# Hybrid attention block: value projection and gates moved into stages of their own, the head turns cut from 24 to 16 units

## What is computed

```python
h = rms_norm(x, norm_mix)
proj = h @ w_in            # q, k, v of 8 "diff" heads, then q, k, v of 8 "fox" heads, then 8 forget logits
# diff: two 64-wide q/k maps a head, each RMS-normed; p = softmax(q1 k1 + alibi) - lam * softmax(q2 k2 + alibi)
#       out = rms_norm(p @ v) * (1 - lambda_init)
# fox:  q and k RMS-normed over 128; logits q k + F[t] - F[s], F = cumsum(log_sigmoid(f_logit + b_forget))
gates = sigmoid(h @ w_gate + b_gate)                       # 2 x 2048 columns
merged = g_diff * (oa @ w_branch_diff) + g_fox * (ob @ w_branch_fox)
x = x + merged @ w_out
h2 = rms_norm(x, norm_mlp)
x = x + relu(h2 @ w_mlp_up) ** 2 @ w_mlp_down              # hidden width 8192
```

## Time and profile before

| what | value |
|---|---|
| time, median of 3 runs | 2764.06 us (2763.19 to 2764.08) |
| the profiled execution's own time | 2764.29 us |
| its span, from the first to the last instruction | 2762.6 us |
| PE busy in it | 2740.2 us, 99% of the span |
| DVE busy | 1704.2 us, 62% |
| ACT busy | 1114.0 us, 40% |
| granted TensorE clock, mean | 0.999 |
| head turns, from the trace | 28.8 to about 695 us, 83.4 us a turn |

### The profile page before, as it was taken

One profiled execution on the slowest core, in us unless ns is written; L12 is line 12 of the kernel. 1 busy time (PEld: TensorE's weight loads), 2 busy tenths in 40 slices (PEclk: granted clock), 3 DMA queues, 4 the chain that ended last, 5 costly groups with the idle time before them and its releaser, 6 DMA issues.

```text
span 2762.6 us, 42063 instructions
## 1 busy us (share of the span) xinstructions
PE 2740.2 (99%) x14920; PEld 2369.3 (86%) x14920; DVE 1704.2 (62%) x2924; ACT 1114.0 (40%) x1565; POOL 39.9 (1%) x65
## 2 busy tenths in 40 slices
PE   8999999999999999999999999999999999999999
PEld 7888888888888888888889999999998888888887
DVE  5666766667655555563478788788874444444443
ACT  5444444444322222233344444444454334334343
POOL 1000000000000000010000000000000000000000
PEclk9999999999999999999999999999999999999999
DMA  5333232222233333334523443434347565565653
GB/s 161 77 77 76 76 76 75 76 73 80 84 92 99 98 94 97 99 103 131 163 95 127 134 130 123 137 127 132 128 148 251 186 229 195 184 232 192 214 203 115
DMA packets 382059, 358.36 MB, mean 130 GB/s; under 512 B 13299, under 2 KB 302134, under 8 KB 382006
## 3 DMA queue, kind: packets, MB, share of 16 engines
q1 hardware_dynamic: 366534, 332.45, 39.0%
q10 hardware_dynamic: 15472, 25.20, 2.4%
HBM read 332.44 MB, written 25.17 MB: 129 GB/s over the span
## 4 chain that ended last, share of the span: by engine, by line
PE 95%; DVE 2%; ACT 1%; issue 1%; DMA 0%; SPq 0%; ACTq 0%; DVEq 0%
PE job L1406 12%; PE job L1409 12%; PE job L1408 12%; PE job L1700 2%; PE scores L1700 2%; PE job L1702 2%; PE job L1704 2%; PE scores L1702 2%; PE scores L1704 2%; PE job L1727 2%; PE job L1729 2%; PE job L1728 2%; PE scores L1727 2%; PE scores L1729 2%; PE scores L1728 2%; PE heads_out L1509 1%
## 5 line engine op out<-in xcount | busy, mean ns | idle before, releaser
L547 ACT ACTIVATE w_hi<-raw 128x512 fp32r<-128x512 f32 x452 | 285.5, 633 | 663.3 <-PE job L1409 560.1
L1406 PE MATMUL job<-a_hi,w_hi 128*128 128x512 f32 x1296 | 519.2, 401 | 0.6 <-DVE w_lo L883 0.6
L1409 PE MATMUL job<-a_hi,w_lo 128*128 128x512 f32 x1296 | 506.2, 391 | 0.0
L1408 PE MATMUL job<-a_lo,w_hi 128*128 128x512 f32 x1296 | 505.2, 390 | 0.0
L883 DVE TENSOR_TENSOR w_lo<-raw,w_hi 128x512 fp32r<-128x512 f32 x452 | 309.3, 688 | 302.6 <-ACT w_hi L547 300.7
L1343 DVE TENSOR_TENSOR w_lo_d<-raw_d,w_hi_d 128x512 fp32r<-128x512 f32 x256 | 176.5, 690 | 368.7 <-ACT w_hi_d L828 368.5
L1253 DVE TENSOR_TENSOR lo<-pair,hi 128x1792 fp32r<-128x1792 f32 x128 | 259.0, 2024 | 108.6 <-ACT hi L749 108.6
L828 ACT ACTIVATE w_hi_d<-raw_d 128x512 fp32r<-128x512 f32 x256 | 162.0, 634 | 405.2 <-PE heads_out L1729 202.6
L749 ACT ACTIVATE hi<-pair 128x1792 fp32r<-128x1792 f32 x128 | 217.9, 1702 | 238.2 <-PE heads_out L1704 118.8
L1409 PEld LDWEIGHTS job<-a_hi,w_lo 128*128 128x128 f32 x1296 | 243.2, 188 | 52.5
L1406 PEld LDWEIGHTS job<-a_hi,w_hi 128*128 128x128 f32 x1296 | 243.6, 188 | 48.0 <-DVE a_lo L1063 1.1
(11 more groups left out here) (328 smaller groups left out, 5828.2 us busy)
## 6 DMA issues: line engine op xcount, KB each, us to landing
pair<-in_w_mlp_up SPq DMA_DIRECT2D x256, 256.0 KB, 3.0
u_raw<-u_rows SPq DMA_DIRECT2D x64, 1024.0 KB, 5.6
raw_d<-in_w_mlp_down SPq DMA_DIRECT2D x128, 512.0 KB, 6.1
raw<-in_w_in SPq DMA_DIRECT2D x98, 512.0 KB, 4.0
raw<-in_w_gate SPq DMA_DIRECT2D x64, 512.0 KB, 4.1
raw<-in_w_out SPq DMA_DIRECT2D x64, 256.0 KB, 3.3
u_rows<-u_out ACTq DMA_DIRECT2D x32, 512.0 KB, 4.4
raw<-in_w_branch_diff SPq DMA_DIRECT2D x16, 512.0 KB, 3.9
```

The source lines that it names most:

```text
L547: nc.scalar.activation(w_hi[:, u % SPLITS], raw[:, slot, part:part + KU], ACT.Copy).then_inc(hi_ready, 1)
L1406: nc.tensor.matmul(result[:, :], w_hi[:, slot, k], act_hi[:, f], start=(n == 0 and k == 0), stop=False)
L1408: nc.tensor.matmul(result[:, :], w_hi[:, slot, k], act_lo[:, f], start=False, stop=False)
L1409: done = nc.tensor.matmul(result[:, :], w_lo[:, slot, k], act_hi[:, f], start=False, stop=(n == units - 1 and k == KU - 1))
```

## The change

- **Layout by the host.** x is handed over twice: as it was and as 16 transposed tiles (`x_tiles`); the small vectors come as one array of columns. PE's transposes of x and of the vectors go.
- **Values and forget logits first, token-major.** The weights' columns of all v heads and the forget logits are done ahead of everything, in 5 groups (`VALUE_COLS`: 512, 512, 344, 344, 344 columns). Here the tokens are the stationary side: a group is 16 units of 12 matmuls (4 blocks of 128 tokens, 3 matmuls each, of 512 or 344 columns), and its four results stand in 4 banks. ACT scales them and stores them to DRAM (`keep_values`, `v_rows`); each head turn loads its two v tiles back (`load_v`). No v is transposed any more. In the shadow of this stage ACT and DVE also build the sums of h that the next stage needs (`combine_x`, `round_combos`, `split_combos`).
- **Gates in a stage of their own.** 28 of the 32 gate tiles are made in 14 pairs by the same 7-for-8 rule as the up projection: 56 units of 42 matmuls of 256 columns. DVE scales a pair's 128x1024 result (`scale_gates`), ACT takes the sigmoid by its own table function and stores the gates to DRAM (`finish_gates`, `g_rows`). The merge loads them back (`load_gates_back`).
- **Head turns of 16 units.** A turn has 4 jobs (q, k of diff, q, k of fox). The steps of the attention keep their unit numbers but for `NORM_STEPS` and `NORM_LENGTH`, and fox now lags by 8 units. The last 4 gate tiles fill the 16 units (TAIL) beside which the last head's attention ends.
- **Merge** has only its 16 × 4 branch units. Merged tiles are rounded and subtracted one by one as they come, and POOL has no part in that any more.
- The output, up and down projections are as before. ScalarE's program has 10 ACT_TABLE_LOAD instructions where it had 3.

```diff
-NORM_STEPS = (4, 8, 24)
-NORM_LENGTH = 4
+NORM_STEPS = ((4, 8, 27), (6, 9))
+NORM_LENGTH = 3
+BIAS_STEP = 12
+X_GROUPS = ((0, 1), (1, 2), (2, 4), (4, 8), (8, 12), (12, 16))
+VALUE_COLS = ((2048, 512), (2560, 512), (5120, 344), (5464, 344), (5808, 344))
...
-    HU, HJ = 6 * JU, 6
-    MERGE = HEADS.then(H * HU, H * HJ)
-    MU, MJ = 2 * JU + 2 * BU, 4
+    HU, HJ = 4 * JU, 4
...
+    TAIL = HEADS.then(H * HU, H * HJ)
+    MERGE = TAIL.then(HU, HJ)
+    MU, MJ = 2 * BU, 2
...
+            sp.dma_start(cols[:, 0:columns.shape[1]], columns).then_inc(params_loaded, 16)
+            load_values(0)
+            load_values(1)
+            load_x(3)
+            load_values(2)
+            load_x(4)
+            load_values(3)
+            load_x(5)
+            for b in range(TB):
+                sp.dma_start(x_tok[:, b], x[0, P * b:P * (b + 1)]).then_inc(x_tok_loaded, 16)
+            sp.dma_start(bforget[:, :], b_forget[0:1, :].broadcast_to([P, NF])).then_inc(bforget_loaded, 16)
+            for half in range(4, VU // 2):
+                load_values(half)
...
+            def value_unit(q, k):
...
+                for b in range(TB):
+                    bank, rows = bank_sets[q % 2][b], slice(P * b, P * (b + 1))
+                    nc.tensor.matmul(bank[:, 0:w], a_hi[:, k, rows], high, start=(k == 0), stop=False)
+                    nc.tensor.matmul(bank[:, 0:w], a_lo[:, k, rows], high, start=False, stop=False)
+                    done = nc.tensor.matmul(bank[:, 0:w], a_hi[:, k, rows], low, start=False, stop=(k == DT - 1))
...
+            sum_pair(0, 0, pairs_g)
+            sum_pair(1, 1, pairs_g)
+            split_pair(0, 0, pairs_g, pair_hi_g)
+            dve.wait_ge(v_kept, TB * len(VALUE_COLS))
...
+            gate_pairs(GATE_PAIRS // 2 - 1, last=True)
+            for n in range(LEAD):
+                split_unit(HEADS, n)
+            combine_early(GATE_PAIRS - 1, 0, blocks_g)
+            combine_late(GATE_PAIRS - 1, 0, blocks_g)
+            scale_gates(GATE_PAIRS - 1)
+            dve.wait_ge(g_stored, 32 * GATE_PAIRS)
```

More of the change, by code:

```diff
@@ L676, in _, with finish_tail @@
                 heads_turn(i, Work(HEADS.unit, HEADS.job, i, HU, HJ))
-            def merge(m, work, last=False):
+            def finish_tail(j):
+                tile_no = TAIL_GATES[j]
+                act.wait_ge(tail_scaled, j + 1)
+                nc.scalar.activation(gate_tail, gate_tail, ACT.Sigmoid,
+                                     bias=cols[:, 2 * DT + tile_no:2 * DT + tile_no + 1]).then_inc(tail_squashed, 1)
+                act.wait_ge(tail_squashed, j + 1)
+                rows = g_rows[P * tile_no:P * (tile_no + 1)].rearrange("p (t s) -> p t s", t=2)
+                for t in range(2):
+                    act.dma_start(rows[:, t], gate_tail[:, 2 * P * (1 - t):2 * P * (2 - t)]).then_inc(tail_stored, 16)
@@ L679, in merge @@
+            def merge(m, slot, work, first=False):
                 for u in range(MU):
                     round_unit(work, u + LEAD)
[L681 to L688 removed]
@@ L710, in _ @@
-            merge(DT - 1, MERGE.then((DT - 1) * MU, (DT - 1) * MJ), last=True)
-            for k in range(2 * BU * 3, DT):
-                round_merged(k)
+                    if u == 0 and not first:
+                        round_merged(m - 1, 1 - slot)
+                    if u == 2 and first:
+                        finish_tail(3)
+            merge(0, 0, MERGE, first=True)
+            merge(1, 1, MERGE.then(MU, MJ))
+            with act.Fori(1, DT // 2 - 1) as i:
+                work = Work(MERGE.unit, MERGE.job, i, 2 * MU, 2 * MJ)
+                for j in range(2):
+                    merge(i * 2 + j, j, work.then(j * MU, j * MJ))
@@ L714, in square_x2 @@
+            for m in range(DT - 2, DT):
+                merge(m, m % 2, MERGE.then(m * MU, m * MJ))
+            round_merged(DT - 1, 1)
             def square_x2(q):
@@ L1209, in _ @@
-            merge(DT - 1, MERGE.then((DT - 1) * MU, (DT - 1) * MJ), last=True)
-            for k in range(2 * BU * 3, DT):
-                split_merged(k)
+                    if u == 0 and first:
+                        scale_tail(3)
+                    if u == 1:
+                        if first:
+                            dve.wait_ge(probs_turned, 2 * TB * H)
+                        take_part(m, slot, 0, work)
+                        if not first:
+                            split_merged(m - 1, 1 - slot)
@@ new lines, in merge @@
+                    if u == MU - 1:
+                        take_part(m, slot, 1, work)
+                dve.wait_ge(parts_ready, m * 2 + 2)
+                nc.vector.tensor_tensor(merged[slot], part_d, part_f, ALU.add).then_inc(merged_ready, 1)
+            merge(0, 0, MERGE, first=True)
+            merge(1, 1, MERGE.then(MU, MJ))
+            with dve.Fori(1, DT // 2 - 1) as i:
+                work = Work(MERGE.unit, MERGE.job, i, 2 * MU, 2 * MJ)
+                for j in range(2):
+                    merge(i * 2 + j, j, work.then(j * MU, j * MJ))
@@ L1213, in add_x2 @@
+            for m in range(DT - 2, DT):
+                merge(m, m % 2, MERGE.then(m * MU, m * MJ))
+            split_merged(DT - 1, 1)
             def add_x2(q):
@@ L1637, in merge @@
[L1637 to L1645 removed]
+                job(work.then(BU, 1), b_hi, b_lo, H, BU)
@@ L1647, in out_unit @@
+            merge(0, MERGE, first=True)
+            merge(1, MERGE.then(MU, MJ))
+            with pe.Fori(1, DT // 2 - 1) as i:
+                work = Work(MERGE.unit, MERGE.job, i, 2 * MU, 2 * MJ)
+                for j in range(2):
+                    merge(i * 2 + j, work.then(j * MU, j * MJ))
+            for m in range(DT - 2, DT):
+                merge(m, MERGE.then(m * MU, m * MJ))
             def out_unit(q, k):
```

1020 lines of the change are left out of this document (592 added, 428 removed).

## The result

| | before | changed |
|---|---|---|
| median | 2764.07 us (2763.19 to 2764.39, 4 runs) | 2801.55 us (2800.28 to 2801.73, 4 runs) |
| span of the profiled execution | 2762.6 | 2799.8 |
| mean granted TensorE clock | 0.999 | 0.988 |

The ratio is 1.0135, 95% interval 1.0118 to 1.0153. The forecast was 2752, with 2722 to 2766 as its range.

The account below looks back on a forecast made before the run. PE, busy 99% of the span, was taken as the bound. Savings of −48.3 us, then +28.7 for head turns, +2.3 and +4.9 for seams, gave −12.4 against the 2762.6 span: 2752, range 2722 to 2766.

Parts of the forecast that it names:

- Fewer and cheaper matmuls: PE's matmul work removed and added in values, forget logits and gates: net −29.7 us, nearly all from Strassen's gates.
- a starved value stage: Rival: in the value stage 16 to 20 units take 0.5 us longer, +10, time 2762; chance 0.12.
- a cheaper matmul of 256 columns: Rival: 256-column matmuls cost 0.1131 us in the gate stage, 16 us less there, time 2736; chance 0.02.
- Start: Kernel start: first matmul at 8.2 us, then 3.5 of waiting on loads; overhead 11.7 against 17.96, −6.3.
- Values to gates: Seam from value stage to gate stage: PE waits while logits, sums and a split finish, +2.3 us, bounds 0 and 5.
- Gates to heads: Seam from gate stage to head turns: late splits and the log and cumulative-sum chain, +4.9 us, bounds 1.4 and 10.
- The holes: PE's idle holes going away: −3.2 us at the output stage's start, −2.1 in the old head turns.
- Head turns: New waits of 4.1 us a turn over an ideal 60.8, in 7 turns: +28.7; bounds 0 and 9 a turn (+63).
- the wait before the widening: Head turn, unit 14: PE waits 3.1 us for VectorE's inversion of the diff output's norm.
- The wait of 0.8 at the product with v: Head turn, unit 7: PE waits 0.8 us for a copy of transposed probabilities behind the diff q's inversion.
- The slower one: Rival: head turns wait on VectorE's inversions more than once, slower from 5.9 us a turn; at 8.1, 2780; chance 0.13.
- The first rival: Head turns absorb their waits because engine queues run ahead: 0.3 us lost a turn, time 2725; chance 0.2.

Follow-up runs that it names:

- experiment 2: Changed kernel with ScalarE's last exp before the four k copies and VectorE's diff-output inversion before the four k subtractions: 2768.14 us.
- experiment 5: Changed kernel with PE doing 14 and 10 spare matmuls of 512 columns in its two waits of a turn, results thrown away: 2784.54 us.
- experiment 1: Changed kernel with VectorE's loop over the head turns written out turn by turn: 2779.68 us.
- experiment 6: Changed kernel with both VectorE's head-turn loop written out and the exp and inversion moved ahead of the k copies and subtractions: 2749.40 us, ratio 0.9948.

## Why the prediction was wrong

The forecast was −12.4 against the span; measured +37.2. The missing 49.6 us lie nearly all in one term.

- **Fewer and cheaper matmuls: right.** 0.225, 0.157 and 0.120 in the windows against 0.2262, 0.1564 and 0.1199. Taken away for −29.7, it is all there, and the rivals of a starved value stage and of a cheaper matmul of 256 columns are both out. In the gate stage VectorE (228.73 of 276) covers its work, as costed at 0. The forecast's reason for the 0.1199, that the weight loads set it because PEld is busy all the time, is not shown: PEld is busy for 74.98 of 75 us beside matmuls of 344 columns too, which take 0.157.
- **Start: right in kind.** I had the first matmul at 8.2 (8.10 measured) and the ninth unit at 33.4 (34.11). Not seen was that its first 13 matmuls run at half speed, +2.7; in the kernel before, PE's transposes of x came first (four of them took 1.06 us at 9.62 and 0.60 at 11.79). The load's wait was smaller for that, 1.4 in place of 3.5. The values end at 190.8 where the sum had 188.7.
- **Values to gates: +2.3 forecast, 4.2 measured.** The wait is 2.2, and some 1.6 are the half clock behind it (13 matmuls 0.21 apart and not 0.12). **Gates to heads: +4.9 forecast.** The waits there are 1.5, 1.4 and 0.8, together 3.7.
- **The holes.** The output stage takes 1262.7 to 1444.3, 181.6 us, against 183.5: −1.9, not −3.2. A wait of 2.1 us at the up stage's start was in the hole and stayed.
- **Head turns: this step failed.** "That is 4.1 a turn, and 7 turns have it: +28.7", over an ideal turn of 60.8. The ideal was right: 61.0 busy at a clock of 1.00. But a turn takes 71.7, so 10.9 a turn, 76 in 7 turns, 48 more than forecast and above the bound of 9 a turn too. Of the parts: the wait before the widening was foreseen, with its place and its chain, 3.1 against 3.8; VectorE's steps from the probabilities to the inversion's end took 7.92 where 7.95 was counted, so the difference lies ahead of them. The wait of 0.8 at the product with v is hardly there; in its place stands one of 2.8 before the transposes at the turn's end, whose cause (VectorE's 2.4 us at the loop's end) was in no row that I had looked at, as it is hidden in the kernel before. And the sum priced a wait at its length. Each brings a spell at half clock, together 4.2 us in the turn shown, a term that the sum put at nothing.
- **The rivals.** The slower one had the right side, and its limit of 5.9 us a turn is near the mark (experiment 2, with turns of 66.8 in the mean, 6.0 over the ideal, is 4 us slower than the kernel before). But it named more late inversions; there is one late inversion, one loop end, and the clock. It had 0.13. The first rival ("the turn absorbs its waits"), 0.2, failed: VectorE has 20 us a turn idle, but not where the chain needs them. That the range was too narrow follows from the bounds: the turn's own upper bound of 9 us was +63, and 2766 left most of that out.

For the clock, the level itself agrees with a page. The matmuls of 512 columns at the start come 0.43 us apart. The Trainium skill, "TensorE: Matmul & The Clock Gate", section "Back-to-back issue gap", gives N/1.2 ns for a matmul at the low level, 427 for 512: the trace agrees. Its section "Why this matters for your kernels" has this level follow an idle gap; experiment 5 agrees, where it goes as soon as PE has no gap.

## What to carry to other kernels

Where PE does everything, price a new wait at its length and at the half clock behind it: here 6.5 us of waits a turn cost 10.7. When a turn is shortened, list for every engine what stands in its queue between two things that PE wants, to each of PE's consumers at that place; here a later due time did not help, another order did, and most of its gain came only with both engines at once. And the end of VectorE's loop was 2.4 us and more without an instruction: place such an end where the engine is early.

## What was not expected of the hardware

- VectorE's loop end takes 2.4 to 2.7 us in the changed kernel, and nothing when written out. PE's own loop over the same turns stays a loop in experiment 1, and no gap of over 0.3 us stands in PE's rows there but the waits for VectorE.
- The granted clock does not fall behind every wait of the same length. In the changed kernel it falls behind all six waits of 2.7 to 3.0. After edit 2 the wait at the turn's end is 2.92, 2.72, 2.74 and 3.01 us in four turns that follow each other; the windows right behind them:

```profile
601.50:605.00 3.50, 3.43 (x13) 2.87 (x14) 3.34 (x10) 1.64 (x3) 0.00 (x0) 0.65 0.35 78
668.50:672.00 3.50, 3.50 (x19) 2.92 (x20) 3.37 (x10) 1.77 (x4) 0.00 (x0) 1.00 0.35 91
735.00:738.50 3.50, 3.50 (x13) 2.92 (x14) 3.35 (x10) 1.76 (x4) 0.00 (x0) 0.60 0.40 93
802.00:805.50 3.50, 3.38 (x18) 2.85 (x19) 3.34 (x10) 1.59 (x3) 0.00 (x0) 1.00 0.31 77
```

  The clock falls in the first and the third. With no wait over 1.7 us (experiment 6) it does not fall in the turns at all.
- Matmuls whose results are thrown away, done in the waits, made the kernel 17 us faster.
